# Latent attention prepared in tiles of 128 rows, norms and v's turn inside the input products, reciprocals spread by TensorE

## The reference, cut to what matters

```python
def hybrid_layer(x, positions, rel_bias, ...):
    h = rmsnorm(x, norm_gain)
    q_a, k_a, v_a, z_a, c_q, c_kv, k_rope, z_b = split(h @ w_in)   # 512 x4, 256, 128, 32, 512
    q_a, k_a = rmsnorm per head of 64
    o_a = dilated_window_attention(q_a, k_a, v_a, rel_bias)        # 8 heads, one table per head
    o_b = latent_attention(c_q, c_kv, k_rope, positions, ...)
    mixed = concat([o_a * silu(z_a), o_b * silu(z_b)])
    return x + mixed @ w_out

def latent_attention(c_q, c_kv, k_rope_in, positions, ...):
    q  = (rmsnorm(c_q)  @ w_uq ).reshape(B, S, 8, 64 + 32)         # nope, rope
    kv = (rmsnorm(c_kv) @ w_ukv).reshape(B, S, 8, 64 + 64)         # k_nope, v
    q_nope, q_rope, k_nope = rmsnorm per head of each part
    k_rope = rope(rmsnorm(k_rope_in), cos, sin)                    # one for all heads
    q_rope = rope(q_rope, cos, sin)
    s = (q_nope @ k_nope.T + q_rope @ k_rope.T) * 96 ** -0.5       # causal
    return softmax(s) @ v
```

## Time and profile before

| | |
|---|---|
| median of three runs | 3308.41 us (3307.94 to 3310.57) |
| profiled execution | 3308.43 us, its span 3306.7 us |
| mean granted TensorE clock | 0.894 |
| PE (matmul) busy | 86% of the span |
| PE weight loads | 67% |
| DVE / ACT / POOL busy | 33% / 22% / 29% |

### The profile page before, as it was taken

One profiled execution on the slowest core, in us unless ns is written; L12 is line 12 of the kernel. 1 busy time (PEld: TensorE's weight loads), 2 busy tenths in 40 slices (PEclk: granted clock), 3 DMA queues, 4 the chain that ended last, 5 costly groups with the idle time before them and its releaser, 6 DMA issues.

```text
span 3306.7 us, 33077 instructions
## 1 busy us (share of the span) xinstructions
PE 2849.9 (86%) x13817; PEld 2215.2 (67%) x13817; DVE 1083.9 (33%) x1368; ACT 713.5 (22%) x942; POOL 951.6 (29%) x627
## 2 busy tenths in 40 slices
PE   5999899986658588679899999999879977788988
PEld 3888688864548386468587888788558855434667
DVE  3100100016664552541333333333320015455541
ACT  3001010125421111100311111111311034545430
POOL 2333132320011021362133232232113217501752
PEclk8999799986678587789899999999889999967999
DMA  3211133320000000342011111111021110000004
GB/s 131 64 45 51 39 95 95 102 70 0 1 0 1 1 1 1 132 143 88 26 45 44 51 44 51 44 45 51 13 89 51 45 48 27 1 15 0 1 14 127
DMA packets 188683, 156.36 MB, mean 47 GB/s; under 512 B 9462, under 2 KB 170201, under 8 KB 188322
## 3 DMA queue, kind: packets, MB, share of 16 engines
q1 hardware_dynamic: 188578, 154.86, 15.3%
HBM read 125.45 MB, written 29.40 MB: 47 GB/s over the span
## 4 chain that ended last, share of the span: by engine, by line
PE 74%; DVE 11%; ACT 6%; POOL 5%; issue 2%; DMA 0%; SPq 0%; DVEq 0%; ACTq 0%; POOLq 0%
PE gp L750 18%; PE gp L751 18%; PE gp L752 18%; POOL att_s L714 2%; PE sm L772 2%; PE gp L1152 1%; POOL att_s_b L714 1%; PE sm L1225 1%; PE sm L1273 1%; POOL merged L702 1%; PE gp L988 1%; PE sm L979 1%; PE sm L868 1%; DVE h_tmp L1680 1%; PE sm L986 1%
## 5 line engine op out<-in xcount | busy, mean ns | idle before, releaser
L750 PE MATMUL gp<-h_hi,w_hi 128*128 128x512 f32 x1984 | 780.8, 394 | 43.3 <-DVE h_lo L1690 43.3
L751 PE MATMUL gp<-h_lo,w_hi 128*128 128x512 f32 x1984 | 777.8, 392 | 0.0
L752 PE MATMUL gp<-h_hi,w_lo 128*128 128x512 f32 x1984 | 777.4, 392 | 0.0
L655 POOL CAST w_hi<-w_raw 128x1024 fp32r<-128x1024 f32 (+1 forms) x173 | 179.8, 1039 | 1446.5 <-PE gp L752 1338.0
L750 PEld LDWEIGHTS gp<-h_hi,w_hi 128*128 128x128 f32 x1984 | 375.7, 189 | 132.3 <-DVE h_lo L1690 41.4
L752 PEld LDWEIGHTS gp<-h_hi,w_lo 128*128 128x128 f32 x1984 | 376.1, 190 | 78.6
L751 PEld LDWEIGHTS gp<-h_lo,w_hi 128*128 128x128 f32 x1984 | 376.2, 190 | 77.2
L657 POOL TENSOR_TENSOR w_lo<-w_raw,w_hi 128x1024 fp32r<-128x1024 f32 (+1 forms) x173 | 412.9, 2387 | 13.9
L1992 DVE SCALAR_TENSOR_TENSOR hid<-gp,col,hid 128x1023 f32<-128x1023 f32 x44 | 56.4, 1283 | 313.2 <-ACT hid L1493 313.2
L750 PE MATMUL gp<-g_hi,w_hi 128*128 128x512 f32 x352 | 139.3, 396 | 22.6 <-DVE hid L1995 14.8
L1493 ACT ACTIVATE hid<-gp,col 128x1024 f32<-128x1024 f32 x44 | 49.2, 1118 | 468.0 <-PE gp L752 468.0
(11 more groups left out here) (408 smaller groups left out, 4211.9 us busy)
## 6 DMA issues: line engine op xcount, KB each, us to landing
w_raw<-in_w_in SPq DMA_DIRECT2D x79, 512.0 KB, 3.9
w_raw<-in_w_up SPq DMA_DIRECT2D x44, 512.0 KB, 3.8
gates_spill<-gate_out SPq DMA_DIRECT2D x32, 512.0 KB, 3.1
gate_in<-gates_spill SPq DMA_DIRECT2D x32, 512.0 KB, 3.6
w_raw<-in_w_down SPq DMA_DIRECT2D x22, 512.0 KB, 3.6
x_back<-x_spill SPq DMA_DIRECT2D x16, 512.0 KB, 4.2
x_tok<-in_x SPq DMA_DIRECT2D x8, 512.0 KB, 8.4
x_spill<-x_t SPq DMA_DIRECT2D x1, 4096.0 KB, 12.4
```

What stands on the lines that cost most here:

```text
L655: pool.tensor_copy(w_hi[:, t % 2, 0:n], w_raw[:, t % 2, 0:n]).then_inc(s["w_high"], 1)
L750: pe.matmul(o, wh, hi[:, k0 + k, c], start=(k == 0), stop=False)
L751: pe.matmul(o, wh, lo[:, k0 + k, c], start=False, stop=False)
L752: mm = pe.matmul(o, wl, hi[:, k0 + k, c], start=False, stop=(k == n - 1))
```

## The change

The change touches the second layer alone.

1. The input products run in another order (`IN2_ORDER`): c_q, c_kv and k_rope first, then q, k, v, z_a, z_b. Each of the first twelve is normed while later products run: ACT squares it, PE sums the squares behind the next product, ACT takes the root, DVE scales. The separate norm stage is gone, and so are the norms of c_q, c_kv and k_rope behind A. k_rope's weights are loaded four times side by side, so that it lies in all four groups of 32 rows. The positions are loaded, and the angles made, in this stage; k_rope is turned here, and v is turned one tile of 128 rows at a time.
2. POOL's multiplication by the reciprocals is gone. PE multiplies the identity by the reciprocals, broadcast over 64 columns, into PSUM beside the unit's output (two matmuls), and DVE multiplies the gate twice, by the output and by that.
3. The latent preparation makes 14 tiles of 128 rows: four of k_nope (two heads each), four of v, which are token-major by taking `ckv` as the matmul's other operand, two of rope (four heads each), four of q_nope.
4. A score of B is two matmuls accumulated in one bank: 64 rows of nope and 32 rows of rope.
5. POOL splits the output products' input while B runs; the splits of c_q and c_kv move from ACT and DVE to POOL.
6. A's bias tables have three places, the first of which is `w_raw`.

The core of the diff:

```diff
-P_OUT = P_UKV + 8
+P_LATENT = P_IN2 + 24
+P_OUT = P_LATENT + 14
 P_END = P_OUT + 8
+
+
+IN2_ORDER = (16, 17, 18, 19) + tuple(range(16)) + (20, 21, 22, 23)
+LATENT = (("k", 0), ("k", 1), ("v", 0), ("k", 2), ("v", 1), ("k", 3), ("v", 2), ("r", 0), ("v", 3), ("r", 1),
+          ("q", 0), ("q", 1), ("q", 2), ("q", 3))
+NORMED = tuple((n, kind, j) for n, (kind, j) in enumerate(LATENT) if kind != "v")
 
+            def split_mix(k):
+                z = (z_a, z_b)[k // 4][:, k % 4, :]
+                pool.tensor_copy(mix_hi[:, k, :], z).then_inc(s["mix_high"], 1)
+                pool.wait_ge(s["mix_high"], k + 1)
+                pool.tensor_tensor(mix_lo[:, k, :], z, mix_hi[:, k, :].bitcast(F32), ALU.subtract) \
+                    .then_inc(s["mix_split"], 1)
...
+            pool.wait_ge(s["p_ready"], P_OUT)
+            for k in range(4):
+                split_mix(k)
+            split_weights(T_OUT)
+            split_weights(T_OUT + 1)
+            for j in range(4):
+                pool.wait_ge(s["at_o_taken"], UNITS + NB * (j + 1))
+                split_mix(4 + j)
+            for t in range(T_OUT + 2, T_END):
                 split_weights(t)
...
+            for n in range(24):
+                whole(T_IN2 + n, P_IN2 + n, h_hi, h_lo)
+                i = n - 1
+                if 0 <= i < 12:
+
+                    pe.wait_ge(s["n2_sq"], i + 1)
+                    if i >= 2:
+                        pe.wait_ge(s["n2_rt"], i - 1)
+                    which = ones if i < 3 else quad_ones if i == 3 else head_ones
+                    for half in range(2):
+                        mm = pe.matmul(sm[:, half, :], which[:, :], nsq[:, HALF * half:HALF * half + HALF],
+                                       start=(i != 1), stop=(i != 0), skip_group_check=True)
+                    mm.then_inc(s["n2_ss"], 1)
+                elif 12 <= i < 16:
...
+                elif i == 16:
+                    pe.wait_ge(s["n2_rt"], 11)
+                    pe.wait_ge(s["n2_q"], 3)
+                    turn_rope(k_rope, 0)
...
-                    pe.wait_ge(s["at_share"], 2 * (u + 1))
+                    pe.wait_ge(s["at_p"], 2 * (u + 1))
...
+                    pe.wait_ge(s["at_root"], u + 1)
+                    for hh in range(2):
+                        pe.matmul(at_share_place()[C * hh:C * hh + C, :], at_small(2, u, hh).to_broadcast([P, C]),
+                                  ident[:, :], start=True, stop=True, skip_group_check=True)
...
+            def latent(n):
+                kind, j = LATENT[n]
+                p = P_LATENT + n
+                if kind == "r":
+                    pe.wait_ge(s["w_split"], T_UQ + 1)
+                    pe.wait_ge(s["q_split"], 2)
+                elif kind == "q" and j:
+                    pe.wait_ge(s["w_split"], T_UQ + 2)
+                pe.wait_ge(s[f"p_free{p % 2}"], frees_before(p))
+                if kind == "k":
+                    mm = product(p, [ring(T_UKV, P * j, P * j + P)], P, ckv_hi, ckv_lo)
+                elif kind == "v":
+                    wh, wl = ring(T_UKV, HALF, 2 * HALF)
+                    for half in range(2):
+                        o, c = gp[:, p % 2, HALF * half:HALF * half + HALF], slice(P * (2 * j + half), P * (2 * j + half) + P)
+                        pe.matmul(o, ckv_hi[:, 0, c], wh, start=True, stop=False)
+                        pe.matmul(o, ckv_lo[:, 0, c], wh, start=False, stop=False)
+                        mm = pe.matmul(o, ckv_hi[:, 0, c], wl, start=False, stop=True)
+                else:
+                    t, c = (T_UQ, P * j) if kind == "r" else (T_UQ, 256) if j == 0 else (T_UQ + 1, P * (j - 1))
+                    mm = product(p, [ring(t, 384 * k + c, 384 * k + c + P) for k in range(2)], P, cq_hi, cq_lo)
+                mm.then_inc(s["p_ready"], 1)
+
...
             def scores_b(j, hh, qb, o, a, m):
-                return pe.matmul(o, qh[:, 2 * j + hh, P * qb:P * qb + P], kh[:, 2 * j + hh, a:a + m],
-                                 start=True, stop=True)
-
-            attention(range(UNITS, 2 * UNITS), scores_b, att_s_b, att_pt_b, v_b)
+                rows = slice(C * hh, C * hh + C)
+                quad = slice(32 * (2 * j + hh) % P, 32 * (2 * j + hh) % P + 32)
+                c = slice(P * qb, P * qb + P)
+                pe.matmul(o, qn[rows, j, c], kn[rows, j, a:a + m], start=True, stop=False)
+                return pe.matmul(o, qr[j // 2][quad, c], k_rope[quad, a:a + m], start=False, stop=True)
...
+                act.activation(dst, ps, ACT.Copy if n < 16 else ACT.Silu).then_inc(s[f"p_free{p % 2}"], 1)
+                i = n - 1
+                if 0 <= i < 12:
+                    act.wait_ge(s["n2_ss"], i + 1)
+                    if i >= 2:
+                        act.wait_ge(s["n2_q"], i - 1)
+                    if i >= 1:
+                        root_of(nrt[:, :], pair(0), BW if i == 1 else P if i == 2 else 32 if i == 3 else C, "n2_rt")
+                if n < 12:
+                    act.wait_ge(s[f"p_free{p % 2}"], frees_before(p) + 1)
+                    act.activation(nsq[:, :], q_2[:, n - 4, :] if 4 <= n < 8 else dst, ACT.Square).then_inc(s["n2_sq"], 1)
...
-                    dve.tensor_tensor(z, z, at_o_place()[:, ::step], ALU.mult).then_inc(s["at_o_taken"], 1)
+                    dve.tensor_tensor(z, z, at_o_place()[:, ::step], ALU.mult).then_inc(s["at_half_gated"], 1)
+                    dve.wait_ge(s["at_half_gated"], u + 1)
+                    dve.tensor_tensor(z, z, at_share_place()[:, ::step], ALU.mult).then_inc(s["at_o_taken"], 1)
...
```

More of the change, by code:

```diff
@@ L1184, in _ @@
             attention(range(UNITS), scores_a, att_s, att_pt, v_2)
-            for j in range(3):
-                wait("c_sq")
-                for half in range(2):
-                    c = slice(HALF * half, HALF * half + HALF)
-                    mm = pe.matmul(sm[:, (0, 0, 2)[j] + half, :], ones[:, :], nsq[:, j % 2, c],
-                                   start=(j != 1), stop=(j != 0), skip_group_check=True)
-                mm.then_inc(s["c_ss"], 1)
-            wait("c_sq")
-            wait("c_root", 2)
@@ L1196, in _ @@
-            for half in range(2):
-                c = slice(HALF * half, HALF * half + HALF)
-                mm = pe.matmul(sm[C:C + 32, half, :], ones[C:C + 32, 0:32], nsq[C:C + 32, 1, c], start=True, stop=True)
-            mm.then_inc(s["c_ss"], 1)
-            def turn_rope(view, place):
-                for half in range(2):
-                    c = slice(HALF * half, HALF * half + HALF)
-                    mm = pe.matmul(place[C:C + 32, c], rope_turn[C:C + 32, :], view[:, c],
-                                   start=True, stop=True)
-                mm.then_inc(s["rot"], 1)
@@ L1218, in _ @@
-            wait("mla_ones")
-            def head_norm(rows, h, place):
-                wait("hn_sq")
-                for half in range(2):
-                    c = slice(HALF * half, HALF * half + HALF)
-                    mm = pe.matmul(sm[0:rows, place + half, :], mla_ones[0:rows, 0:rows], nsq_b[0:rows, h % 2, c],
-                                   start=True, stop=True)
-                mm.then_inc(s["hn_ss"], 1)
-            for z in range(2):
-                pe.wait_ge(s[f"p_free{z}"], frees_before(P_UKV))
@@ L1278, in turn_out @@
+            attention(range(UNITS, 2 * UNITS), scores_b, att_s, att_pt, v_b)
             def turn_out(d):
@@ new lines, in _ @@
+            for i, (n, kind, j) in enumerate(NORMED):
+                p = P_LATENT + n
+                alone = i and NORMED[i - 1][0] < n - 1
+                if alone:
+                    head_root(i - 1)
+                act.wait_ge(s["p_ready"], p + 1)
+                if i >= 2:
+                    act.wait_ge(s["hn_ss"], i - 1)
+                act.activation(hsq[:, i % 2, :], gp[:, p % 2, :], ACT.Square).then_inc(s["hn_sq"], 1)
+                if i and not alone:
+                    head_root(i - 1)
@@ L1662, in _ @@
+            head_root(len(NORMED) - 1)
+            attention(range(UNITS, 2 * UNITS), att_s, att_pt)
             for d in range(KT):
@@ new lines, in _ @@
+            for i in range(1, 4):
+                n2_normed(i)
+            wait("pos_in", 16)
+            wait.after(dve.tensor_copy(ang[:, :], pos_i[:, :]))
+            wait.after(dve.tensor_scalar(ang[:, :], ang[:, :], freq[:, :], None, ALU.mult))
+            wait.after(dve.tensor_scalar(turns[:, :], ang[:, :], 1.0 / (2 * math.pi), ROUND, ALU.mult, ALU.add))
+            wait.after(dve.tensor_scalar(turns[:, :], turns[:, :], -ROUND, None, ALU.add))
+            for part in TURN:
+                wait.after(dve.scalar_tensor_tensor(ang[:, :], turns[:, :], -part, ang[:, :], ALU.mult, ALU.add))
@@ L2186, in _ @@
+            for z in range(2):
+                dve.wait_ge(s[f"p_free{z}"], frees_before(P_OUT))
+            wait("causal")
+            attention(range(UNITS, 2 * UNITS), lambda u, hh: causal, att_s, att_pt, z_b, 1)
             for d in range(KT):
```

547 lines of the change are left out of this document (215 added, 332 removed).

## The result

The changed kernel takes 3386.82 us (median of four runs, 3378.72 to 3389.38), the kernel before 3309.14 in the same comparison (3307.94 to 3310.57): ratio 1.023, 95% interval 1.0212 to 1.0249. It is 78 us slower. The profiled execution was the fastest of the four, 3378.72 us with a span of 3377.0. So the profile, on which the terms stand, explains 70 us of the 78; the four runs lie 10.7 us apart, those of before 2.6.

A forecast was written before the change was run, and what follows sets the result against it. It took PE to bound the input products and mainly B, with A partly on POOL. Terms +22 - 29 - 21 - 61 + 188 - 5 = +94 on 3308.43 us gave 3402, stated as 3400, range 3275 to 3490.

The forecast's parts named there:

- Input stage, +22: Input products: 13 fp32 sums and k_rope's turn enter PE's queue at 1.71 us each, 22 us more.
- Norms, -29: Norm stage of q and k: its 30.4 us go, one copy and a handover stay, 29 us less.
- A, -21: Windowed attention: POOL's shares go, PE and DVE take small extra work, 133 us, 21 less.
- Latent preparation, -61: Stage before latent attention: 158 us become 14 tiles taking 97 us, 61 less.
- third of the way: Latent preparation: its time taken as 97 us, between 82 at full clock and 130 with PE's part at half.
- B, +188: Latent attention: passes double, 192 shape changes cost 0.20 us each, scores run at half clock; 162 to 350 us.
- The fifth that I gave back: B: about a fifth of the 122.9 us half-clock cost returned, as stretches start at the clock they find; 98 left.
- Output stage, -5: Output products: 8 us of wait for splits goes as POOL splits under B, less 3 for clock; 5 us less.
- The 3 us that I allowed for the clock: Output stage: allowance of 3 us because PE may begin at half clock after B.
- Start, 0: Kernel start: two DMAs and three POOL operations fewer, eight POOL ones moved; no change, 0 us.
- (c): Rival for B: nope of one head overlaps rope of the other, B 152 us, total 3204; chance 0.12.
- (b): Rival for B: shapes serialize but the clock stays full, B 252 us, total 3304; chance 0.14.

The follow-up runs named there:

- e4b: e1_grouped with A's reciprocals multiplied in by POOL again, latent weight splits put behind them: 3257.38 us against e1_grouped's 3231.3.
- e8_pairs: e5_unit_groups with the gains loaded through ACT, latent tiles ordered in pairs and each pair's sums behind it: 3198.36 us, ratio to before 0.9667.
- e2_full_rows: The changed kernel with both matmuls of a B score over all 128 rows instead of 64 and 32 (scores wrong): 3261.54 us.
- e1_grouped: The changed kernel with B's score matmuls ordered nope, nope, rope, rope per 512 columns: 3231.3 us, ratio to before 0.9767.
- e5_unit_groups: e1_grouped with B's scores grouped over the whole unit, all nope then all rope: 3219.35 us, ratio to before 0.973.
- e3_rope_64_rows: The changed kernel with B's rope matmul over 64 rows instead of 32, old order nope, rope, nope, rope (scores wrong): 3216.2 us.

## Why the prediction was right

**Input stage, +22.** Right. From first to last copy the stage grew by 22.7 us. Twelve neighbours are 12.64 us apart instead of 10.88, so a sum costs 1.76 and not 1.71.

**Norms, -29.** Right: 30.40 became 1.20.

**A, -21.** Right: -22.0, and e4b shows that it is POOL's.

**Latent preparation, -61.** Right: -64.6 (93.4 for 97). The chain that I had written out is there, with 9.7 us a round where I had 8.4 at full clock, and a mean clock of 0.83. That it hangs on one slot of `gp`, and that another order loosens it, I hadn't seen (e8_pairs). The "third of the way" to half clock was a guess that came near.

**B, +188.** Right in mechanism, 22 us too large. The part at full clock held: 0.19 to 0.20 us at each change, no overlap of nope and rope, passes doubled. e2_full_rows has the same passes at nearly full clock and none of the 192 changes; 212.4 + 192 x 0.20 = 251 is my estimate from it for B at full clock, where I had 252. The clock then cost about 328.4 - 251 = 77 us, and not 98. This is the term that was mis-sized, and its make-up was wrong: I had the scores at half clock and the rest at full. Added up from start to start, the score matmuls take 210.5 us; in e2_full_rows they take 131.8, which is 170 with the changes. Transposes, outputs and reciprocals take 117.8, against 80.3 there. So the clock took some 40 us from the scores, where I had 98, and 37 from the rest, where I had none. The clock comes back in the middle of scores and is still down in the transposes behind them. Fourteen of these take 3.25 us in the changed kernel and 1.77 in e2_full_rows:

```profile
3003.14 3.25 PE L1200 MATMUL gp<-ident,att_s 128*128 128x128 f32 x14
```
```profile
3030.08 1.77 PE L1200 MATMUL gp<-ident,att_s 128*128 128x128 f32 x14
```

That two errors in opposite directions left only 21 us is luck. The fifth that I gave back for the clock that a stretch finds at its start had no row behind it, and no run shows it. From 2950 to 2980 the clock was at half throughout (0.50 in each stretch of 10 us); from there on it went up and down.

**Output stage, -5.** It was -7.6. The first result is taken 11.2 us after B (3281.33) where it was 19.0. The 3 us that I allowed for the clock weren't lost, since the granted clock was 1.00 from 3265 on, in B's last 5 us and just behind them.

**Start, 0.** Wrong: 4.5 in this profile, about 3 on the mean of the eight. I had counted two DMAs fewer, and not what a broadcast one takes to issue (0.56 to 0.74 us against 0.25 to 0.28).

Of the rivals, (c) is what one other order of the same matmuls gives: e1_grouped has B at 181.7 and e5_unit_groups at 171.4, against 152 for (c), which had no price for the changes between nope and rope, and with its terms adding up to 151 left 1 us for start and end where the forecast's B has 7. (b), full clock in the order as it is, did not occur in any run.

The Trainium skill's page "TensorEngine Tiling (Array Packing)", section Key Properties, says that a change of tiling mode drains TensorE. The runs agree: 0.19 to 0.20 us between 64 and 32 rows, nothing between matmuls of one shape. The Trainium skill's page "TensorE: Matmul & The Clock Gate", Part 3, says that small-K matmuls in distinct row groups run concurrently; here they did so only beside one of their own shape (e1_grouped, e3_rope_64_rows).

## What to carry to other kernels

A matmul over few rows costs as much as one over all (0.86 us for two passes of 512 columns at full clock, with 32 rows or 128) and can cost the clock as well, so splitting a contraction in two doubles its passes unless the parts run side by side. They do that only next to a matmul of the same shape: group by shape first, then by head or bank, and look at the starts of neighbouring matmuls, since the busy share hardly tells (PE was busy for 99% of B in the changed kernel and for 95% in e1_grouped, which is 147 us shorter). Move work off an engine where another waits long for it (A's reciprocals, 25 us) and not where the wait is no longer than the work that replaces it (B's, 7.4 us against 9.0), and when two PSUM slots alternate, list which tiles share one.

## What the runs showed of the hardware

I had not expected that two halves of the array each go on with their own matmuls across one that stands between them in the program (e3_rope_64_rows). Two kernels with the same passes and no gap between them ran at a mean granted clock of 0.98 with 128 rows in use and 0.69 with 32; with 64-row matmuls side by side it was 0.96. At half clock a change of shape costs more: starts 2.00 us apart for two passes of 0.86 leave 0.28. Each of the six DMAs with a broadcast source (0.5 KB) took SP 0.56 to 0.74 us to issue, a plain one of 0.5 KB (`kv_c_gain`) 0.25; their target pattern has a dimension more too, and which of the two costs the time is not shown. At the start of the kernel the six of them moved everything behind by about 3 us.
